# Projecting V of the dilation-16 attention group for two head pairs in 256-column products

## The reference, cut to what matters

```python
hn = _rmsnorm(x, norm_g)
proj = jnp.einsum('bsd,de->bse', hn, w_in)                   # [B,S,9216]
q, k, v, z_a, hc, gb, gc, z_b, g = jnp.split(proj, _split_points(), axis=-1)
for gi in range(3):                                          # dilation 1, 4, 16
    o, l = _dilated_band_attention(q[:, :, gi], k[:, :, gi], v[:, :, gi], dil, radius, slopes[gi])
attn = jnp.einsum('gbsh,gbshd->bshd', jax.nn.softmax(lse, axis=0), outs)
a = jnp.einsum('bsc,cd->bsd', jax.nn.silu(z_a) * attn, w_attn_out)
conv = conv_w[0] * up[:, :-2] + conv_w[1] * up[:, 1:-1] + conv_w[2] * up[:, 2:]
c = jnp.einsum('bsc,cd->bsd', jax.nn.silu(z_b) * (gb * conv), w_conv_out)
merged = jax.nn.sigmoid(g_a) * a + jax.nn.sigmoid(g_c) * c
y = _rmsnorm(x + jnp.einsum('bsd,de->bse', merged, w_o), final_g)
```

## Time and profile before

| | |
|---|---|
| median of 3 runs | 1510.78 us (1510.16 to 1510.82) |
| the profiled execution | 1509.57 us |
| its span on the slowest core (core 0) | 1507.7 us |
| spans of all cores | 1501.7 to 1507.7 us |
| mean granted clock of TensorE | 0.997 to 0.998 of 2.4 GHz |
| busy: PE, DVE, ACT, POOL | 97%, 58%, 46%, 13% of the span |

### The profile page before, as it was taken

One profiled execution on the slowest core, in us unless ns is written; L12 is line 12 of the kernel. 1 busy time (PEld: TensorE's weight loads), 2 busy tenths in 40 slices (PEclk: granted clock), 3 DMA queues, 4 the chain that ended last, 5 costly groups with the idle time before them and its releaser, 6 DMA issues.

```text
span 1507.7 us, 32357 instructions; the slowest of 8 cores (1501.7 to 1507.7 us)
## 1 busy us (share of the span) xinstructions
PE 1462.3 (97%) x14195; PEld 870.8 (58%) x14364; DVE 870.5 (58%) x1072; ACT 686.4 (46%) x1032; POOL 198.5 (13%) x357
## 2 busy tenths in 40 slices
PE   8999999999999999999999999999999999999997
PEld 7656766767667544444445676656766444444443
DVE  4883382482563598444476447556485696533456
ACT  5764464564664324333342556565564321222222
POOL 2640000000000103011131100000000101000011
PEclk9999999999999999999999999999999999999999
DMA  9761232221322344334387413323231333222157
GB/s 287 193 167 21 51 59 42 59 43 29 64 38 57 57 91 107 62 71 80 62 263 223 102 27 53 77 45 71 39 67 23 64 50 55 40 32 42 22 191 256
DMA packets 53614, 127.42 MB, mean 85 GB/s; under 512 B 12001, under 2 KB 13153, under 8 KB 53474
## 3 DMA queue, kind: packets, MB, share of 16 engines
q0 software_dynamic: 24336, 44.31, 19.2%
q1 hardware_dynamic: 29138, 81.03, 16.7%
HBM read 145.97 MB, written 23.66 MB: 113 GB/s over the span
## 4 chain that ended last, share of the span: by engine, by line
PE 87%; DMA 4%; DVE 3%; POOL 2%; issue 2%; ACT 1%; SPq 0%; POOLq 0%; ACTq 0%; DVEq 0%
PE ps L431 79%; PE ps L443 8%; DMA Y<-xw 2%; DVE Y L395 1%; DVE Y L386 1%; DMA Y<-wblk 1%; ACT Y L382 1%; POOL stat L574 1%; DMA Y<-fgvec 1%; POOL stat L405 1%; PE ps L458 1%; ACT Y L418 0%; SPq L462 0%; DVE Y L419 0%; POOL wbf L462 0%
## 5 line engine op out<-in xcount | busy, mean ns | idle before, releaser
L431 PE MATMUL ps<-hnT,wbf 128*128 128x512 bf16 (+1 forms) x4301 | 880.2, 357 | 24.8 <-issue 11.5
L431 PEld LDWEIGHTS ps<-hnT,wbf 128*128 128x128 bf16 x4448 | 401.3, 98 | 449.1 <-ACT Y L418 5.0
L382 ACT ACTIVATE Y<-ps 128x1024 bf16<-128x1024 f32 (+2 forms) x296 | 242.5, 863 | 206.8 <-PE ps L431 147.5
L418 ACT ACTIVATE Y<-ps 128x512 bf16<-128x512 f32 (+2 forms) x348 | 203.3, 591 | 268.7 <-PE ps L431 251.2
L386 DVE TENSOR_TENSOR Y<-ps,Y 128x512 f32<-128x512 f32 (+1 forms) x200 | 154.1, 807 | 285.3 <-PE ps L443 265.1
L395 DVE SCALAR_TENSOR_TENSOR Y<-Y,ps 128x512 f32<-128x512 f32 x192 | 131.3, 685 | 211.6 <-PE ps L431 170.3
L431 PE MATMUL ps<-wbf,hnT 128*128 128x128 bf16 x3744 | 231.5, 222 | 0.6 <-DVE Y L386 0.6
L431 PEld LDWEIGHTS ps<-wbf,hnT 128*128 128x128 bf16 x3744 | 225.1, 123 | 11.6 <-DVE Y L386 0.8
L462 POOL DMA_DIRECT2D wbf<-wblk x151 | 84.9, 563 | 913.0 <-PE ps L431 900.0
L382 ACT ACTIVATE Y<-ps,cf 128x512 f32<-128x512 f32 x128 | 87.4, 685 | 191.1 <-PE ps L431 184.3
L382 ACT ACTIVATE Y<-Y 128x1024 bf16<-128x1024 f32 x80 | 84.5, 1056 | 113.4 <-DVE Y L395 85.6
(11 more groups left out here) (29 smaller groups left out, 414.6 us busy)
## 6 DMA issues: line engine op xcount, KB each, us to landing
Y<-xw SPq DMA_DIRECT2D x80, 512.0 KB, 5.8
wbf<-wblk POOLq DMA_DIRECT2D x151, 256.0 KB, 4.7
y<-Y SPq DMA_DIRECT2D x32, 512.0 KB, 4.6
Y<-wblk POOLq DMA_DIRECT2D x18, 256.0 KB, 5.1
Y<-wblk SPq DMA_DIRECT2D x7, 512.0 KB, 13.4
et<-etab SPq DMA_DIRECT2D x8, 384.0 KB, 5.7
cv<-Y SPq DMA_DIRECT2D x4, 768.0 KB, 5.0
Y<-cv SPq DMA_DIRECT2D x4, 768.0 KB, 5.9
```

The source lines that it names most:

```text
L382: R.add("act", [lambda e: e.activation(out=out.a, in_=in_.a, func=func, scale=scale, **kw)], c_act(in_.n) + (0.2 if accum is not None else ...
L418: return e.activation(out=out.a, in_=in_.a, func=AF.Copy)
L431: fns = [(lambda e, m=m: e.matmul(m[0].a, lhsT=m[1].a, rhs=m[2].a, start=m[3], stop=m[4])) for m in mms]
```

## The change

For dilation 16 the even head pair of two now projects V for both. Its weight group loads two V blocks into neighbouring slots, and `vals2` streams both (256 columns) against each stationary token tile; a piece makes two tiles, 2 * 8 products, in one bank. The bank is copied out twice: the even pair's half into its own `vb`, the odd pair's half into one of five small stage buffers (`vpS`), which are stored to a new DRAM tensor `vp` on SP's queue. The odd pair's unit, three units later, has no V pieces and no V weights: its `setup` reads all its tiles back from `vp` in one DMA, ones included, and the mask pattern is copied over it afterwards. The stages take the place of two of the seven `xn0` buffers for late halo tiles. Keys of two chunks are dealt out in another place, two halo tiles come one step earlier, and in the merge of half 1 POOL is given two memsets and five operations on buffers of their own at 96 to 102 KB.

```diff
@@ build_program
+    vp_d = nc.dram_tensor("vp", [2 * 128, 32 * VB_T], BF16)
...
+        xnl = xn0[:5]
+        vpS = [yb(108 + 0.75 * i, 768, BF16) for i in range(5)]
+        vpF = yb(108, 3840, F32)
+        vpc = {"i": 0}
...
                 grp = [c + g * 512 + hp * 128 for c in (C_Q, C_K, C_V)]
+                if g == 2:
+                    grp[2:] = [None] if hp % 2 else [grp[2], grp[2] + 128]
...
-                if j not in js:
+                if j not in js or col is None:
...
-            return ln_tok(t, fetch(t, buf), xn0, gb0, jk0, bank)
+            return ln_tok(t, fetch(t, buf), xnl if late else xn0, gb0, jk0, bank)
@@ setup
-                o = vbF[par].ap(t0 * VB_T // 2 + 32, ones + [[1, 32]])
-                R.add("pool", [lambda e: e.memset(o.a, 1.0019378662109375)], 0.3 + 0.001 * o.n, [], [o])
+                if g == 2 and hp % 2:
+                    t0 = 16 * h
+                    o = vb_b.cols(t0 * VB_T, (32 - t0) * VB_T)
+                    row = hp // 2 * 128 * 32 * VB_T
+                    dma("sp", o.a, bass.AP(vp_d, row + t0 * VB_T, [[32 * VB_T, 128], [1, (32 - t0) * VB_T]]),
+                        [dram_ref("vp", (hp // 2, t)) for t in range(t0, 32, 2)], [o], 5.0 if h == 0 else 2.5)
+                else:
...
+                    parts = [vbF[par].ap(t0 * VB_T // 2 + 32, ones + [[1, 32]])]
+                    if g == 2:
+                        parts.append(vpF.ap(32, [[VB_T // 2, 10], [1, 32]]))
+                    for o in parts:
+                        R.add("pool", [lambda e, o=o: e.memset(o.a, 1.0019378662109375)], 0.3 + 0.001 * o.n, [], [o])
@@ pieces
+            def vals2(t, t0):
+
+                def f():
+                    bk = next_bank()
+                    bv = bankv[bk]
+                    mms = [(bv.cols(j * 256, 256), hnT.ap(kt * HST + hc(t + j), [[16, 128]]),
+                            wbf.ap(sv * 1024 + kt * 128, [[1024, 2], [1, 128]]), kt == 0, kt == 7, 128)
+                           for j in range(2) for kt in range(8)]
+                    pe(mms, [bv.cols(0, 512)])
+                    stage = vpS[vpc["i"] % 5]
+                    vpc["i"] += 1
+                    for x, dst in enumerate((vb_b.ap(t0 * VB_T, [[VB_T, 2], [128, 2], [1, 64]]),
+                                             stage.ap(0, [[VB_T, 2], [128, 2], [1, 64]]))):
+                        copy(dst, bv.ap(128 * x, [[256, 2], [64, 2], [1, 64]]))
+                    o = stage.cols(0, 2 * VB_T)
+                    dma("sp", bass.AP(vp_d, hp // 2 * 128 * 32 * VB_T + t0 * VB_T, [[32 * VB_T, 128], [1, 2 * VB_T]]), o.a,
+                        [o], [dram_ref("vp", (hp // 2, t0))], 0.4)
+                return f
...
-                    by_chunk[0 if (x, c) != (1, 3) else 2].append(keys(b0 + 2048 * x + 512 * c, 2048 * x + 512 * c))
-                for x, c in sorted(order):
-                    by_chunk[2].append(vals([(b0 + 2048 * x + 4 * c + j, 16) for j in range(4)], 16 * x + 4 * c, 1))
+                    by_chunk[2 if h == 0 and (x, c) in ((0, 0), (1, 3)) else 0].append(keys(b0 + 2048 * x + 512 * c, 2048 * x + 512 * c))
+                for x, c in sorted(order) if hp % 2 == 0 else ():
+                    for r in (4 * c, 4 * c + 2):
+                        by_chunk[2].append(vals2(b0 + 2048 * x + r, 16 * x + r))
@@ merge
+                if h == 1 and dt_ == 2:
+                    pa, pb, po = (yb(96 + 2 * i, 2048, F32) for i in range(3))
+                    for o, v in ((pa, 2.5), (pb, -1.0)):
+                        o = o.cols(0, 512)
+                        R.add("pool", [lambda e, o=o, v=v: e.memset(o.a, v)], 0.8, [], [o])
+                    for n, op in ((256, ALU.pow), (64, ALU.pow), (512, ALU.mult), (512, ALU.mult), (512, ALU.mult)):
+                        tt(po.cols(0, n), pa.cols(0, n), pb.cols(0, n), op, eng="pool")
@@ halo
-                for t in halos[4 + 2 * c:6 + 2 * c] if c < 4 else halos[(12, 13, 15, 16)[c - 4]:(13, 15, 16, 16)[c - 4]]:
+                for t in halos[4 + 2 * c:6 + 2 * c] if c < 4 else halos[(12, 14, 16, 16)[c - 4]:(14, 16, 16, 16)[c - 4]]:
```

More of the change, by code:

```diff
@@ L648, in setup @@
                 nf = NFIRST[g]
-                ones = {0: [[VB_T // 2, 17 - h]], 1: [[5 * VB_T // 2, 4], [VB_T // 2, 5 - h]],
-                        2: [[VB_T // 2, 32 - 16 * h]]}[g]
-                t0 = {0: h, 1: h, 2: 16 * h}[g]
-                o = vbF[par].ap(t0 * VB_T // 2 + 32, ones + [[1, 32]])
-                R.add("pool", [lambda e: e.memset(o.a, 1.0019378662109375)], 0.3 + 0.001 * o.n, [], [o])
+                if g == 2 and hp % 2:
[5 more added lines that the diff above has]
+                else:
+                    ones = {0: [[VB_T // 2, 17 - h]], 1: [[5 * VB_T // 2, 4], [VB_T // 2, 5 - h]],
+                            2: [[VB_T // 2, 32 - 16 * h]]}[g]
+                    t0 = {0: h, 1: h, 2: 16 * h}[g]
+                    parts = [vbF[par].ap(t0 * VB_T // 2 + 32, ones + [[1, 32]])]
[3 more added lines that the diff above has]
+                        R.add("pool", [lambda e, o=o: e.memset(o.a, 1.0019378662109375)], 0.3 + 0.001 * o.n, [], [o])
                 m0, mdims = tile_dims(g, h == 0, VB_T)
```

## The result

The changed kernel takes **1526.27 us** (median of 4 runs, 1525.32 to 1527.87) against 1510.8 for the kernel before in the same comparison: a ratio of 1.0105, 95% interval 1.0085 to 1.0125. It is 15.5 us slower, where 1501.0 had been forecast and 1523 was the upper end of the range. In some executions the cores of a die show a lower granted clock and the time is longer; the medians given here leave those executions out.

A forecast was written before the change was run, and what follows sets the result against it. TensorE, busy 97% of the span, was taken to bound the kernel. -14.9 + 3.6 + 1.0 + 0.5 = -9.8 us against the profiled 1509.57 gave 1499.8; the runs' median, 1.2 higher, made it 1501.0 us, range 1493 to 1523.

The forecast's parts named there:

- Part 4: Merge of half 1: the 256-column power on POOL takes 8.4 us, with 23 us free: hidden, costs nothing.
- Rival A: POOL's power outlasts its 23 us, the HC load is late, PE stands in half 1: 1523 us; chance 0.24.
- Part 1: V of dilation 16: 768 products of 256 columns at 111.3 ns, 85.5 us in place of 100.4; 14.9 us saved.
- rival C: Paired V: the slow pace stays with the columns, 128.0 ns, saving 2.1 us instead of 14.9: 1513.8; chance 0.05.
- whatever the stationary pattern: V products: the skill's 134 and 262 cycles taken to hold for any stationary side, leaving a saving of 1.9 us.
- Part 2: Attention filler leaves units 4 and 10; half 1's light units, two pieces a step, give back 3.6 us.
- Part 3: V's detour through DRAM: stores hidden, DVE's mask copy waits for the reads; 1.0 us for all four.
- The sign that DVE would wait for the reads under 3 us: Next profile, V's reads from DRAM: DVE waits under 3 us for them if the forecast is right.
- The light unit: Next profile, half 1: units 4 and 10 near 20.5 us if the forecast is right.
- Rival B: Starved light units and late reads take their upper ends, 8.4 + 8 instead of 4.6 us: 1512.8; chance 0.08.
- The small edits: Second V block loaded one unit earlier, a fourth load issue in the start stage: 0.5 us; halo tiles and keys covered.

The follow-up runs named there:

- e3_pow128: The changed kernel with the first power on POOL on 128 columns in place of 256: 1504.84 us, ratio 0.9962 against the kernel before.
- e5_half0: The changed kernel without the powers, V paired in half 0 only: 1503.31 us, ratio 0.9952 against the kernel before.
- e1_no_pool: The changed kernel without its two memsets and five POOL operations, paired V kept: 1504.03 us, ratio 0.9957 against the kernel before.
- e11_even_deal: The changed kernel without POOL operations, odd pairs' mask copy on POOL, half 1's light units dealt two pieces every step: 1499.11 us, 0.9924 against the kernel before.
- e10_true_power: The changed kernel with all POOL operations, the planner told their measured durations: 1511.72 us, ratio 1.0001 against the kernel before.

## Why the prediction was wrong, step by step

**The step that failed is Part 4**, the price of the 256-column power on POOL. It was "8.4 us: hidden, nothing", the geometric middle of 0.8 and 89; it lasts 41.28. What hung on that number held. The place, right behind the last fused product and ahead of the HC load, is the one that was read from the planner's 0.42 us. The 23 us that it might last were right: 20.8 is free, 31.0 leaves a hole of 6.6. Rival A is what happened, with its sign (a hole in the conv stage of half 1, ended by a weight DMA, POOL busy before it). The rows could not give the price: a power of one column at 567 ns and a memset at 1 ns a column left a factor of a hundred, and the chance of A, 0.24, was what an even spread over that factor gives. What the middle hid is that the outcome is decided by a threshold at 23 us, and that a power past it costs up to 66 us (89 - 23) while one below it gains nothing. The upper bound's reasoning, that the 347 ns over an add recur with each column, was the nearer one: the slope is 160 ns. The middle was 33 us short, and what it put at nothing cost some 20. One reading beside it was wrong and harmless: in the next 28 us POOL does have loads to issue, five times from 1194.62 to 1220.49 in the kernel before, but with the second power and the products among them `e3_pow128` lost nothing.

**Rival A's own price was short by the clock.** The hole was priced, the products after it were not: at the 1.2 GHz level 14 of them take 3 us more, after 17.3 us of rest and also after 6.6. With it and the true 41.28, A's sum is (41.3 - 23) + 3 - 9.8 = +11.5 us, 1522; with the paired V's true -6.8, 1525, against 1526.27 measured. The two isolated prices of the POOL block agree with that: 1526.27 - 1504.03 = 22.2 us in the kernel after and 19.8 in the kernel before, around the trace's 20.3.

**Part 1 held**: 110.5 ns where 111.3 was taken. PE's weight loads of the first paired V of half 0:

```profile
358.55 13.97 PEld L436 LDWEIGHTS ps<-wbf,hnT 128*128 128x128 bf16 x128
372.69 1.18 PEld L448 LDWEIGHTS ps<-Y 64*128 64x128 bf16 x48 [0.17 <-issue]
```

(372.69 - 358.55)/128 = 110.5 ns. The slow pace does not go with the columns (rival C falls), and the idle before the group behind is 0.17 us. The Trainium skill, "TensorE: Matmul & The Clock Gate", section "Back-to-back issue gap", has 262 cycles for 256 columns, at 2.4 GHz an estimate of 109 ns: the trace agrees there to about 1%. Its 134 cycles for 128 columns are an estimate of 56 ns, and the 64.0 of the earlier trace rows are not that. That page of the Trainium skill gives both for a product on its own and by its columns alone; "whatever the stationary pattern" was the prediction's reading. The saving that it left, 1.9 us, is refuted by the 7.3 us of `e5_half0`.

**Parts 2 and 3: the right waits, too small.** Predicted for the paired V: -9.8; measured: -6.8. At 110.5 ns the width itself saves 4 x 16.4 - 512 x 0.1105 = 9.0 us in half 0 and 4 x 8.7 - 256 x 0.1105 = 6.5 in half 1. Of the latter up to 1.3 us were not V's: the 8.7 of Part 1 hold a wait of 0.33 us for DVE, once in each of the four units. Half 0 returned 7.3 of its 9.0. In half 1 two losses were shown. The deal costs 3.7 us in the trace and 3.3 in the time, where Part 2 took 3.6; but the place is the one that the prediction had put into its upper bound, a last step with no filler of its own, rather than a little in each step, so the agreement of the size is luck. Steps of two pieces took 4.8 us with the even deal, not the 5.12 that Part 2 took from the earlier trace rows. The order of the deal was 2, 3, 3, 0 and not 3, 3, 2, 0. The late reads cost 2.9 us in the trace and 1.0 to 1.7 in the time, where Part 3 took 1.0. It had looked for that wait in half 0, at the 1.5 MB read, and for 0.75 MB estimated 5.9 us against a planner's 4.95. Issued together with the V carry on SP's queue the small read lands in 8.1 (DMA issues of the page of the kernel after: count, KB each, median us from issue to landing):

```profile
Y<-vp SPq DMA_DIRECT2D x2, 1536.0 KB, 10.4
Y<-vp SPq DMA_DIRECT2D x2, 768.0 KB, 8.1
```

The sign that DVE would wait for the reads under 3 us failed with it: DVE waits 11.3 us for them in `e1_no_pool`. With both losses taken out, `e11_even_deal` gains 11.6 us of the width's 15.5. By the table 1.8 us stay away in half 0 (440.0 - 432.7 = 7.3 of 9.0) and 1.5 in half 1 (5.0 of 6.5); what holds them there was not pinned down by a run. The light unit was forecast at 20.5 us, four steps of the 5.12 in the earlier trace rows; it took 25.4, then 23.9 without the read's wait and 20.9 with the even deal. Rival B was so a part of the truth in half 1, without deciding the sign, and PE stood before filler products more than before fused ones.

The small edits left no trace that could be told from the runs' spread: the first fused product stands at 81.64 us in the kernel before, and between 80.4 and 82.0 in the paired versions. The additional load issue there was not tried by itself.

## What to carry to other kernels

An operation whose result nothing reads still has a place in its engine's queue: ask what is issued behind it, how many microseconds it has, and whether its duration has ever been seen at that width. Where the bounds of that duration straddle the free time, the price is not the middle of the bounds but the chance of passing the threshold times what lies behind it, the slow clock after the hole included. And work taken out of one unit shortens the kernel only where the unit keeps filler for each of its steps and no engine that PE depends on stands in its queue for a transfer: half 1 gave nothing at first, and 5.0 of its 6.5 us once the mask copy was off DVE and the pieces were dealt evenly.

## What was not expected of the hardware

The power on POOL was linear in its columns: 0.35 us and 0.16 us for each column from 64 to 256 of them, with nothing gained by width, some 155 times a memset's column. That line gives 0.51 us for one column, near the 567 ns of the earlier trace rows: the single column's 567 ns were within a factor of four of the pace of many, 160. And TensorE's granted clock was at the 1.2 GHz level after a rest of 6.6 us as after one of 17.3, for 5.5 and 6.0 us of products. In `e10_true_power` it was 1.00 through a rest of 4.7 us and the first 0.8 us of products after it (1226.2 to 1231.6), and 0.50 from 1232.6 to 1238.6. The waits of 1 to 2 us in the light units are in slices whose clock digit is a 9.
